# Moving the split activations of a float32r two-block network by 128 bytes in SBUF

## The chip, the cores and the metric

The kernel runs on one core of one Trainium2 chip. The metric is the device time of one execution in microseconds (us), lower is better. Everything is float32 in memory; the large products run on the matrix engine as float32r, in three passes.

## The reference: two transformer-like blocks

One sequence of 256 tokens of width 1024 goes through two blocks, with two layers each. The parts that matter here are all products of an activation with a weight:

```python
# first block, for each of 2 layers
h = h + 0.5 * (1 + mod2) * swiglu(u, ffn1_wg, ffn1_wu, ffn1_wd)     # 1024 -> 2816 -> 1024
proj = u @ w_in                      # retention, stick-breaking attention, mamba2
h = h + (1 + mod5) * (concat([y_ret, y_sb, y_ssm]) @ w_out)
h = h + 0.5 * (1 + mod8) * swiglu(u, ffn2_wg, ffn2_wu, ffn2_wd)
# second block, for each of 2 layers
proj = h @ w_in                      # neighbourhood, MLA and GQA attention, three gates
x = x + g_m * (merged @ w_out)
x = x + g_f * ((silu(gate) * up) @ ffn_w_down)
```

Each u is an RMS norm of the state, scaled and shifted by vectors that come from a conditioning vector times the matrices ada_w (the "ada" work).

## The kernel before

**Layout.** Activations stand transposed: 128 features on the partitions, the 256 tokens along the free dimension, one tile of 256 columns (1024 bytes) for each 128 features. A weight tile is 128 x 128 (512 bytes per partition) and is the stationary operand; the activation tile of 256 columns is the moving one. The exception is `tokens()`, for values that must stand untransposed: there a 128-column piece of the activation is stationary and the weights move.

**Three passes.** Each number is split into a high float32r part and a low one (the rest). `mm3` adds three matmuls into one PSUM tile: high weight by high activation, high by low, low by high. All of them are recorded at line L647 (`mm`). Each matmul has a weight load of its own.

**Weights.** 310 fills of up to 1 MB come through SP's queue into `ring`, a ring of 3 slots of 2048 floats per partition. A fill holds two "grains" of 1024 floats. For each grain ScalarE writes the high part into `high` (L1127) and VectorE the low part into `low` (L1561); both rings have 4 grains. TensorE works through the grains in order, 24 matmuls for a grain of eight 128 x 128 tiles. A fill is issued when the fill three before it has been split.

**Split activations.** The moving operands stand in five buffers, each the high parts followed by the low parts:

- `u_split`: the normed input of every projection, and of gate and up in the feed-forward stages
- `hid`: the hidden tiles of a feed-forward stage (22 high, 22 low)
- `xa` and `xr`: what goes into w_out of the first block (`into_acc`)
- `merged`: what goes into w_out of the second block (`into_acc`, the same function and the same weight tiles)

`u_split` ends at the byte `TOP`; `region`, a work area of `REGION` floats that the stages share, lies below it. `xa`, `xr`, `merged` and `hid` are views into `region` at fixed offsets:

```python
REGION = 16672
XA_AT, XR_AT, HID_AT = 12576, 6176, REGION - 2 * FT * T
TOP = 229312
...
self.u_split = self.sb("u_split", 2 * KT * T, F32R, TOP - 8 * KT * T)
base = TOP - 8 * KT * T - 4 * REGION
self.region = self.sb("region", REGION, F32, base)
self.xa = self.sb("xa", 16 * T, F32R, base + 4 * XA_AT)
```

**Stages.** In order: f1, m1, f2 for each layer of the first block, a final norm, then m2, f3 for each layer of the second, and an output norm. A feed-forward stage is 22 units of gate and up (48 matmuls each) and 528 matmuls of down. The mixers m1 and m2 put small float32 matmuls of attention and scan (the "side" pieces) between their projections. VectorE also does the ada products (L1543) at a fixed rate per grain.

The functions that the diff touches, with the profile's line numbers:

Of the kernel before, what the change touches and what calls it, by code (L numbers as in the profile page):

```python
# [24 lines left out]
T = 256  # L25
TT = T // P
LAYERS = 2
FF = 2816
FT = FF // P
CHUNK = 64  # L30
HD = 128
SSM_H, SSM_P, SSM_G, CONV = 8, 64, 2, 4
EPS = 1e-6
TRI = T + P
# [36 lines left out]

FIRST = 2 * KT
FIRST_AT = TT * D
REGION = 16672
XA_AT, XR_AT, HID_AT = 12576, 6176, REGION - 2 * FT * T


TOP = 229312

# [2 lines left out]
class Fill:  # L84


    def __init__(self, *parts):
        self.parts = parts
        _, _, _, self.rows, _, self.cols = parts[0]
        self.width = sum(rows * cols for _, _, _, rows, _, cols in parts)  # L90
        self.grains = []
# [334 lines left out]
class Memory:  # L426


    def __init__(self, nc, ctx):
        self.nc, self.at = nc, (nc.sbuf_base + 31) // 32 * 32  # L430
        names = ["pe", "act", "dve", "pool", "params", "ident", "const", "c", "cb", "x", "bias", "store", "const2"] \
            + [f"fill{i}" for i in range(SLOTS)] + [f"ada{i}" for i in range(ADA_SLOTS)] + [f"first{i}" for i in range(FIRST // 2 - 1)]
        self.sems = {n: ctx.enter_context(nc.semaphore(f"s_{n}")) for n in names}
        self.ring = self.sb("ring", SLOTS * SLOT)
        self.high = self.sb("high", GRAINS * GRAIN, F32R)
        self.low = self.sb("low", GRAINS * GRAIN, F32R)
        self.ada_ring = self.sb("ada_ring", ADA_SLOTS * D)
        self.cst = self.sb("cst", max(C1_W, C2_W))
        self.par = self.sb("par", BASE_C + PC_W)
        self.h = self.sb("h", KT * T)  # L440
        self.tmp = self.sb("tmp", 5 * 512)
        self.rope_t = self.sb("rope_t", 2 * 512)
        self.sil = self.sb("sil", 2 * T)
        self.rs = self.sb("rs", 2 * 512)
        self.ones = self.sb("ones", P)
        self.eps = self.sb("eps", 1)
        self.cond = self.sb("cond", 2 * D)
        self.sums = self.sb("sums", KT * len(JOBS))
        self.mods = self.sb("mods", KT * len(JOBS))
        self.gates = self.sb("gates", KT)  # L450
        self.gcol = self.sb("gcol", KT)
        self.dts = self.sb("dts", 8 * 16)
        self.keys = self.sb("keys", 4 * T)
        self.stat = self.sb("stat", 24)
        self.u_split = self.sb("u_split", 2 * KT * T, F32R, TOP - 8 * KT * T)
        base = TOP - 8 * KT * T - 4 * REGION
        assert self.at <= base, (self.at, base)
        self.region = self.sb("region", REGION, F32, base)
        self.xa = self.sb("xa", 16 * T, F32R, base + 4 * XA_AT)
        self.xr = self.sb("xr", 8 * T, F32R, base + 4 * XR_AT)  # L460
        self.merged = self.sb("merged", 16 * T, F32R, base)
        self.hid_split = self.sb("hid", 2 * FT * T, F32R, base + 4 * HID_AT)
        self.psum = ctx.enter_context(nc.psum_tensor("bank", [P, 8 * 512], F32))
        self.banks = [self.psum[:, i * 512:(i + 1) * 512] for i in range(8)]
        self.hv = tiles(self.h, KT)
        self.uh, self.ul = tiles(self.u_split, KT), tiles(self.u_split, KT, T, KT * T)
        self.squares, self.normed = tiles(self.tmp, 4), tiles(self.tmp, 4, T, 1024)
        self.hid = tiles(self.hid_split, FT), tiles(self.hid_split, FT, T, FT * T)
        self.x = self.reg(0, TT, D)


        self.xp = self.reg(0, 8, T + CONV - 1)
        self.rqk, self.sv, self.sg = self.reg(0, 4, 512), self.reg(2080, TT, 512), self.reg(3104, 4)
        self.sqk, self.sz, self.ry = self.reg(4128, 2, 512), self.reg(5152, 4), self.reg(5152, 2)
        self.xbc, self.xdt = self.reg(XR_AT, 8), self.reg(8224, TT, 512)
        self.cbm = [self.region[:, 9248 + g * TRI:9248 + (g + 1) * TRI] for g in range(SSM_G)]
        self.rr = [self.region[:, 10016 + i * TRI:10016 + (i + 1) * TRI] for i in range(2)]
        self.dec = [self.region[:, 10784 + i * TRI:10784 + (i + 1) * TRI] for i in range(2)]
        self.sy = self.reg(11552, 4)
        self.y_sb = tiles(self.xa, 8), tiles(self.xa, 8, T, 8 * T)  # L480
        self.y_ret = tiles(self.xr, 4), tiles(self.xr, 4, T, 4 * T)
        self.tb = [self.tmp[:, i * TRI:(i + 1) * TRI] for i in range(6)]
        self.dt8 = [self.dts[:, i * 16:(i + 1) * 16] for i in range(8)]


        self.qa, self.va = self.reg(0, 2), self.reg(1024, TT)

        self.ka, self.gkz = two(self.keys[:, :], 4), self.reg(512, 2)
        self.kr, self.cqn, self.ckvn = self.reg(2048, 1), self.reg(2560, 2), self.reg(3072, 1)
        self.qb, self.kb, self.vm = self.reg(3328, 4), self.reg(4352, 4), self.reg(5376, TT)  # L490
        self.gq, self.gk, self.gv = self.reg(5888, 4), self.reg(6912, 1), self.reg(7424, TT, P)

        self.gate2, self.o = self.reg(7680, 24), self.reg(13824, 8)
        self.total = self.reg(7680, 8)
        self.head_squares = [self.sil, self.rs[:, 512:1024]]
        self.inner = tiles(self.sil, 2)[:, 0, :], tiles(self.sil, 2)[:, 1, :]
        self.na_bias = self.region[:, 11776:13824]
        self.S = [self.tmp[:, i * 512:(i + 1) * 512] for i in range(3)]
        self.PT = [self.tmp[:, 1536:2048], self.tmp[:, 2048:2560], self.region[:, 15872:16384]]
        self.merged_hl = tiles(self.merged, 8), tiles(self.merged, 8, T, 8 * T)  # L500
# [62 lines left out]
def tiles(t, n, width=T, at=0):  # L563
    return t[:, at:at + n * width].rearrange("p (n w) -> p n w", n=n)


def two(ap, n=2):
    return ap.rearrange("p (n w) -> p n w", n=n)
# [1750 lines left out]
```

## Time and profile before

| what | value |
|---|---|
| time, median of 3 runs | 2097.65 us (2094.57 to 2100.68) |
| the profiled execution's own time | 2095.65 us |
| its span, first to last instruction | 2093.9 us |
| mean granted TensorE clock | 0.979 of full speed |
| TensorE matmul busy | 95% of the span, 15720 instructions |
| VectorE, ScalarE, GpSimd busy | 69%, 49%, 6% |
| DMA | 466.35 MB, mean 223 GB/s |

A matmul's duration in the trace (279 ns, say) is longer than the distance between two of them, since they are pipelined: what a stretch costs is read from the starts. A busy share near 100% therefore says that TensorE had no gap, not how fast it went.

### The profile page before, as it was taken

To read this page: it belongs to the slowest core of one execution; us is meant where nothing else is said; L and a number is where in the kernel's file an instruction comes from. 1 tells how busy PE (TensorE), PEld (TensorE's weight loads), DVE (VectorE), ACT (ScalarE), POOL (GpSimd) and SP (SyncE) were. 2 spreads that over 40 slices of the span, in tenths; PEclk is the share of its full clock that TensorE was granted. 3 is DMA by queue.
4 is the path that set the end of the run, shared out by engine and by line. 5 is a ranking of instruction groups with operands and counts; after the bars stand their busy time and mean duration, and the time that the engine had idled before them with its cause. 6 is when DMAs were issued, how large, how long until landed. Compare 5 with 4: busy or idle time off the path is not lost.

```text
span 2093.9 us, 37422 instructions
## 1 busy us (share of the span) xinstructions
PE 1988.4 (95%) x15720; PEld 1936.4 (92%) x15720; DVE 1437.9 (69%) x2203; ACT 1021.2 (49%) x1568; POOL 117.2 (6%) x113
## 2 busy tenths in 40 slices
PE   3999899989999999999999979998999899999999
PEld 3999899989999999999899979998999899989998
DVE  6767687877677676968776757665777776656554
ACT  3444556454545444664644455443545454525443
POOL 0000002200000000022000010000000100000000
PEclk8999999999999999999999989999999999999999
DMA  8777565567786775755577745455677664554552
GB/s 347 263 253 288 185 231 193 191 220 251 253 290 212 253 275 212 252 199 208 208 267 254 278 165 202 164 211 201 211 257 277 220 207 170 194 202 168 192 184 100
DMA packets 83848, 466.35 MB, mean 223 GB/s; under 512 B 9440, under 2 KB 9568, under 8 KB 44512
## 3 DMA queue, kind: packets, MB, share of 16 engines
q1 hardware_dynamic: 46496, 326.00, 43.5%
q10 hardware_dynamic: 37184, 137.97, 18.2%
q8 instruction: 123, 2.02, 0.4%
q14 instruction: 45, 0.37, 0.0%
HBM read 462.88 MB, written 1.05 MB: 222 GB/s over the span
## 4 chain that ended last, share of the span: by engine, by line
PE 85%; DVE 7%; ACT 4%; DMA 1%; issue 1%; POOL 1%; ACTq 0%; DVEq 0%
PE bank L647 84%; DVE low L1561 2%; DMA region<-ada 1%; DVE ada_ring L1543 1%; ACT high L1127 1%; DVE u_split L1604 1%; PE bank L916 1%; DVE tmp L1599 1%; ACT u_split L1165 0%; POOL region L2047 0%; DVE region L1975 0%; DVE region L1930 0%; ACT rs L1148 0%; PE bank L1055 0%; ACTq L1495 0%
## 5 line engine op out<-in xcount | busy, mean ns | idle before, releaser
L647 PE MATMUL bank<-u_split,high 128*128 128x256 f32 x6464 | 1171.2, 284 | 47.9 <-DVE u_split L1604 41.8
L647 PEld LDWEIGHTS bank<-u_split,high 128*128 128x128 f32 x6464 | 1000.2, 190 | 58.7 <-DVE u_split L1604 35.4
L1561 DVE TENSOR_TENSOR low<-ring,high 128x1024 fp32r<-128x1024 f32 (+1 forms) x600 | 732.6, 1229 | 393.4 <-issue 237.9
L647 PE MATMUL bank<-u_split,low 128*128 128x256 f32 x3232 | 909.6, 281 | 0.0
L1127 ACT ACTIVATE high<-ring 128x1024 fp32r<-128x1024 f32 (+1 forms) x600 | 602.5, 1045 | 108.3 <-PE bank L647 96.6
L647 PEld LDWEIGHTS bank<-u_split,low 128*128 128x128 f32 x3232 | 612.5, 190 | 0.4
L647 PE MATMUL bank<-hid,high 128*128 128x256 f32 x2112 | 373.4, 279 | 0.0
L647 PEld LDWEIGHTS bank<-hid,high 128*128 128x128 f32 x2112 | 322.4, 188 | 0.0
L1543 DVE SCALAR_TENSOR_TENSOR ada_ring<-ada_ring,cond 128x1024 f32<-128x1024 f32 x242 | 298.0, 1232 | 0.0
L647 PE MATMUL bank<-hid,low 128*128 128x256 f32 x1056 | 294.8, 279 | 0.0
L647 PEld LDWEIGHTS bank<-hid,low 128*128 128x128 f32 x1056 | 198.1, 188 | 0.0
L1193 ACT ACTIVATE sil<-bank 128x256 f32<-128x256 f32 x132 | 50.7, 384 | 276.2 <-PE bank L647 276.1
L1199 ACT ACTIVATE hid<-sil 128x256 fp32r<-128x256 f32 x132 | 55.4, 420 | 95.9 <-DVE sil L1651 95.9
L2017 POOL TENSOR_TENSOR tmp<-tmp 128x256 f32<-128x256 f32 x36 | 26.6, 740 | 1243.9 <-ACT tmp L1181 1243.9
L1181 ACT ACTIVATE tmp<-h 128x256 f32<-128x256 f32 x48 | 20.0, 418 | 136.4 <-DVE h L1639 136.4
L647 PE MATMUL bank<-region 128*128 128x256 f32 (+2 forms) x312 | 70.1, 351 | 4.6 <-DVE xa L1672 3.7
L647 PE MATMUL bank<-high,u_split 128*128 128x256 f32 (+1 forms) x384 | 68.1, 279 | 1.0 <-ACT region L1228 1.0
L647 PE MATMUL bank<-region,ring 128*128 128x256 f32 (+1 forms) x304 | 66.8, 380 | 0.0
L1599 DVE SCALAR_TENSOR_TENSOR tmp<-h,gcol,rs 128x256 f32<-128x256 f32 x88 | 40.8, 479 | 36.5 <-ACT rs L1151 36.5
L647 PEld LDWEIGHTS bank<-region 128*128 128x128 f32 (+1 forms) x312 | 53.6, 189 | 13.1 <-DVE xa L1672 4.3
L647 PEld LDWEIGHTS bank<-region,ring 128*128 128x128 f32 (+1 forms) x304 | 56.7, 187 | 9.1 <-ACT region L1473 0.5
L647 PEld LDWEIGHTS bank<-high,u_split 128*128 128x128 f32 x384 | 59.0, 189 | 1.3 <-ACT region L1335 1.2
(186 smaller groups left out, 1650.1 us busy)
## 6 DMA issues: line engine op xcount, KB each, us to landing
ring<-stream SPq DMA_DIRECT2D x302, 1024.0 KB, 5.5
ada_ring<-ada ACTq DMA_DIRECT2D x242, 512.0 KB, 4.3
region<-ada ACTq DMA_DIRECT2D x7, 1024.0 KB, 22.3
ring<-stream SPq DMA_DIRECT2D x4, 640.0 KB, 4.6
region<-na_bias ACTq DMA_DIRECT2D x2, 1024.0 KB, 5.5
ring<-stream SPq DMA_DIRECT2D x4, 512.0 KB, 4.2
cst<-const ACTq DMA_DIRECT2D x1, 1600.0 KB, 21.0
cond<-cond SPq DMA_DIRECT2D x2, 512.0 KB, 7.6
```

The costliest lines, as they stand in the source:

```text
L647: return pe.e.matmul(out, lhs, rhs, start=start, stop=stop, skip_group_check=True)
L916: t = pe.e.transpose(b[:, k * T + a * P:k * T + (a + 1) * P], m.S[p][:, a * T + k * P:a * T + (k + 1) * P], m.c2("ident"))
L1127: act.e.activation(hi, src, ACT.Copy).then_inc(*act.done(("high", n)))
L1181: act.e.activation(m.squares[:, square_slot(d), :], m.hv[:, d, :], ACT.Square) \
L1193: act.e.activation(g, m.banks[act.bank("hid", f, n)][:, 0:T], ACT.Silu).then_inc(*act.done(("silu", f, n)))
L1199: act.e.activation(m.hid[0][:, n, :], g, ACT.Copy).then_inc(*act.done(("hid_high", f, n)))
L1543: dve.e.scalar_tensor_tensor(out=w, in0=w, scalar=1.0, in1=m.cond[:, block * D:(block + 1) * D], op0=ALU.mult, op1=ALU.mult, accum_out=m.s ...
L1561: dve.e.tensor_tensor(lo, src, hi.bitcast(F32), ALU.subtract).then_inc(*dve.done(("low", n)))
L1599: dve.e.scalar_tensor_tensor(out=out, in0=m.hv[:, d, :], scalar=gain[:, d:d + 1], in1=m.rs[:, 0:T], op0=ALU.mult, op1=ALU.mult).then_inc(* ...
L1604: dve.e.scalar_tensor_tensor(out=m.ul[:, e, :], in0=m.normed[:, e % 4, :], scalar=m.mod(shift)[:, e:e + 1], in1=m.uh[:, e, :].bitcast(F32) ...
L2017: pool.e.tensor_tensor(total, total, m.squares[:, square_slot(d), :], ALU.add) \
```

## The change

It moves buffers and nothing else. Only addresses change; every engine's instructions, their order, their shapes and their waits are the same, line by line (one blank line less in the file puts each line number one lower).

```diff
-REGION = 16672
-XA_AT, XR_AT, HID_AT = 12576, 6176, REGION - 2 * FT * T
-
-
-TOP = 229312
+REGION = 16704
+XA_AT, XR_AT, HID_AT = 12608, 6208, REGION - 2 * FT * T
+
+TOP = 229184
...
-        self.xbc, self.xdt = self.reg(XR_AT, 8), self.reg(8224, TT, 512)
-        self.cbm = [self.region[:, 9248 + g * TRI:9248 + (g + 1) * TRI] for g in range(SSM_G)]
-        self.rr = [self.region[:, 10016 + i * TRI:10016 + (i + 1) * TRI] for i in range(2)]
-        self.dec = [self.region[:, 10784 + i * TRI:10784 + (i + 1) * TRI] for i in range(2)]
-        self.sy = self.reg(11552, 4)
+        self.xbc, self.xdt = self.reg(XR_AT, 8), self.reg(8256, TT, 512)
+        self.cbm = [self.region[:, 9280 + g * TRI:9280 + (g + 1) * TRI] for g in range(SSM_G)]
+        self.rr = [self.region[:, 10048 + i * TRI:10048 + (i + 1) * TRI] for i in range(2)]
+        self.dec = [self.region[:, 10816 + i * TRI:10816 + (i + 1) * TRI] for i in range(2)]
+        self.sy = self.reg(11584, 4)
```

The start of each buffer, in bytes from the start of a partition, and what is left of it after division by 256 and by 1024. Every tile of an activation lies a multiple of 1024 bytes behind its buffer's start, every 128-column weight tile a multiple of 512.

| buffer | before | mod 256 | mod 1024 | after | mod 256 | mod 1024 |
|---|---|---|---|---|---|---|
| high (weights) | 41088 | 128 | 128 | 41088 | 128 | 128 |
| low (weights) | 57472 | 128 | 128 | 57472 | 128 | 128 |
| u_split | 212928 | 192 | 960 | 212800 | 64 | 832 |
| hid | 167872 | 192 | 960 | 167744 | 64 | 832 |
| xa | 196544 | 192 | 960 | 196416 | 64 | 832 |
| xr | 170944 | 192 | 960 | 170816 | 64 | 832 |
| merged, region | 146240 | 64 | 832 | 145984 | 64 | 576 |

The distance of an activation from the weights, modulo 256, was 192 - 128 = 64 for all but `merged` and becomes 64 - 128 = -64, that is 192, for all. The parts of `region` at fixed offsets (`sv`, `sz`, `o`, `gate2` and others) move by 256 bytes; `xbc`, `xdt`, `cbm`, `rr`, `dec` and `sy` move by 128.

## Rows read from the trace of the kernel before

**Rows 1.** The page's first part: engine, busy us (share of span), instructions.

```profile
PE 1988.4 (95%) x15720; PEld 1936.4 (92%) x15720; DVE 1437.9 (69%) x2203; ACT 1021.2 (49%) x1568; POOL 117.2 (6%) x113
```

**Rows 2.** Longest pieces of the chain that ended last: start us, us, what.

```profile
41.28 188.34 PE bank L647 x1584
...
430.70 10.74 PE bank L647 x64
444.12 188.30 PE bank L647 x1584
643.90 181.19 PE bank L647 x1536
...
1018.57 9.36 PE bank L647 x64
1030.60 188.33 PE bank L647 x1584
...
1467.16 188.37 PE bank L647 x1584
...
1894.28 188.34 PE bank L647 x1584
```

**Rows 3.** Timeline of TensorE in m1's w_out: start us, us, what.

```profile
393.23 0.28 PE L647 MATMUL bank<-xa,low 128*128 128x256 f32 x1
393.35 0.40 PE L647 MATMUL bank<-xa,high 128*128 128x256 f32 x2
...
398.53 0.28 PE L647 MATMUL bank<-xa,low 128*128 128x256 f32 x1
```

**Rows 4.** The same in m2's w_out.

```profile
1447.82 0.28 PE L647 MATMUL bank<-merged,low 128*128 128x256 f32 x1
1447.93 0.39 PE L647 MATMUL bank<-merged,high 128*128 128x256 f32 x2
...
1460.74 0.28 PE L647 MATMUL bank<-merged,low 128*128 128x256 f32 x1
```

**Rows 5.** Matmuls by tile, whole span: duration ns min/median/max, first and last start.

```profile
L647 PE MATMUL bank<-hid,high x2112: 279/279/280, 167.3 to 2082.2; 128*128 128x256 f32 x192
L647 PE MATMUL bank<-xa,high x256: 278/279/681, 392.6 to 1009.9; 128*128 128x256 f32 x128
L647 PE MATMUL bank<-merged,high x256: 276/276/582, 1431.9 to 1887.7; 128*128 128x256 f32 x128
```

**Rows 6.** Tile u_split moving, windows 45:166, 885:902 and 337:342.5.

```profile
L647 PE MATMUL bank<-u_split,high x687: 279/279/280, 44.8 to 166.0; 128*128 128x256 f32 x172
...
L647 PE MATMUL bank<-u_split,high x93: 276/276/363, 885.5 to 901.9; 128*128 128x256 f32 x93
...
L647 PE MATMUL bank<-u_split,high x32: 276/276/363, 337.2 to 342.5; 128*128 128x256 f32 x32
```

**Rows 7.** Tile u_split stationary (tokens), windows 934:948, 873:882 and 1675:1684.

```profile
L647 PE MATMUL bank<-high,u_split x64: 276/276/369, 934.7 to 947.8; 128*128 128x256 f32 x64
...
L647 PE MATMUL bank<-high,u_split x53: 281/281/281, 872.8 to 882.0; 128*128 128x256 f32 x53
...
L647 PE MATMUL bank<-high,u_split x32: 279/281/281, 1677.1 to 1682.7; 128*128 128x256 f32 x32
```

**Rows 8.** Busy time by windows: window, us, engines, clock, DMA share, GB/s.

```profile
45.00:165.00 120.00, 120.00 (x1021) 120.00 (x1020) 83.38 (x120) 60.37 (x89) 0.00 (x0) 1.00 0.71 251
170.00:228.00 58.00, 58.00 (x495) 58.00 (x494) 41.98 (x53) 25.09 (x30) 4.45 (x6) 1.00 0.74 268
...
840.00:964.00 124.00, 119.37 (x966) 116.55 (x966) 100.18 (x166) 72.75 (x102) 15.68 (x15) 1.00 0.62 226
```

**Rows 9.** Waits of SP's own queue in 60:160: us in total, times, longest.

```profile
SPq L350 <- DVE low L1561: 92.7, 35, 3.8
```

**Rows 10.** The chain by line, in 237:375, 375:431, 964:1018 and 1225:1427.

```profile
by line: PE bank L647 78.4%; DVE low L1561 3.8%; ACT L1228 1.9%; DVE ada_ring L1543 1.7%; ACT high L1127 1.5%; issue 1.4%; ACT L1231 0.9%; ACT L1238 0.9%; ACT region L1228 0.9%; ACT region L1323 0.9%; DVE region L1753 0.8%; DVE region L1747
...
by line: DVE low L1561 25.2%; DVE ada_ring L1543 16.8%; issue 9.5%; ACT high L1127 7.1%; POOL region L2047 5.3%; DVE rope_t L1786 3.3%; ACT xa L1259 3.1%; DVE region L1801 2.9%; DVE region L1759 2.9%; DVE region L1794 2.8%; ACT xr L1300 2.6
...
by line: DVE low L1561 29.1%; DVE ada_ring L1543 12.7%; issue 10.5%; ACT high L1127 7.3%; POOL region L2047 5.5%; DVE rope_t L1786 3.4%; ACT xa L1259 3.2%; DVE xa L1672 3.1%; DVE region L1801 3.0%; DVE region L1759 3.0%; DVE region L1794 2.
...
by line: PE bank L647 89.4%; PE bank L916 3.5%; DVE u_split L1604 1.5%; DVE tmp L1599 1.4%; ACT L1139 0.6%; DVE low L1561 0.6%; ACT u_split L1165 0.5%; issue 0.4%; DVE region L1975 0.3%; DVE region L1930 0.3%; ACT region L1440 0.3%; ACT h L
```

## The prediction

> **What bounds the kernel now.** I read the page first. TensorE is busy for 95% of the span, VectorE for 69%, ScalarE for 49% [rows 1]. The longest pieces of the chain that ended last are six feed-forward stages, in each of which nothing but matmuls stands on the path: five of 1584 matmuls in 188.3 us and one, cut a little shorter, of 1536 in 181.19 [rows 2]. The last is 118.0 ns a matmul; the others come to 118.9 with their start. A busy engine without gaps can still be slow, so the question is what one matmul costs, and whether it costs the same from every buffer. For that I read the timeline at the two places where the same function (`into_acc`) works with the same weight tiles on different activations.
>
> - From `xa`, a triple of matmuls (one low row each) comes 15 times between 393.23 and 398.53 [rows 3]: 5.30 / 45 = 117.8 ns a matmul.
> - From `merged`, it comes 38 times between 1447.82 and 1460.74 [rows 4]: 12.92 / 114 = 113.3 ns.
>
> The difference is 4.4 ns, or 3.8%, with the engine full in both. The duration of one matmul is a marker for the two paces: 276 ns in `merged`, 279 and more in `xa`, and in all 2112 of `hid` [rows 5], whose minimum is 279. So every down product runs at the slow pace. Gate and up do too: 687 matmuls from 45 to 166 with a minimum of 279 [rows 6].
>
> **The rule I take from it.** `xa`, `xr`, `hid` and `u_split` stand 64 bytes above the weights modulo 256; `merged` alone stands 64 below. The change gives the four the place of `merged`, modulo 1024 too (832), so each new pairing of a moving tile and a stationary one has a precedent in this trace. It is not a pure function of the address: `u_split` at its old place also ran at 276 ns in some stretches, as 93 matmuls at 885 and 32 at 337 [rows 6]. A timeline of the whole span gives about 420 such matmuls among 3360 of the mixers' projections, and none in the feed-forward stages. So there are two paces, a stretch falls into one of them when it starts, and the address sets the odds: at the old place some 70 stretches between two breaks, of which about one in seven ran fast, in whole or in part; at the place of `merged`, four stretches, all fast within two triples of their start, two of them after a start at the low clock. For `tokens()` the roles are swapped (weights move at 128, `u_split` is stationary at 192, so the moving operand is 64 below as in `merged`): 276 ns at 934, but 281 at 873 and at 1677 [rows 7]. Counted out, some 410 of 560 were fast. This is what keeps me from certainty.
>
> What a page says goes against the change. The Trainium skill's "SBUF — State Buffer" (Who interferes with whom) gives TensorE two independent read ports, one for the moving operand and one for weight loads, and says that it never waits on anyone; its "TensorE: Matmul & The Clock Gate" (Back-to-back issue gap) makes a warm gap of N/2.4 + 2.5 ns, an estimate of 109.2 for 256 columns, without a word on addresses. By them the change would be worth nothing. This trace shows neither that gap nor one gap for all buffers, and the measurement decides; what is left of the rule is a rival below.
>
> **The sum, by part.** Price per matmul that goes from slow to fast: 4.4 ns. Its bounds: 0 if the pace doesn't depend on the place; no more than 4.4 from any row of a 128 x 128 by 256 matmul, since 113.3 is the fastest pace a long stretch shows; and on the other side a small loss, since 281 ns [rows 7] against 279 [rows 5] is the slowest marker that any full stretch shows. I take 4.4, as `merged` is the nearest row: same function, same weights, same residue.
>
> - Feed-forward, six stages: 6 x 1584 = 9504 matmuls x 4.4 = 41.8 us, all on the path [rows 2]. The cover: VectorE is busy 83.4 of 120 us in gate and up and 42.0 of 58 in down [rows 8]; with 4% less time that is 72% and 75%. DMA share is 0.71 to 0.74 at 251 to 268 GB/s, which would be some 260 to 279. SP's queue spends 92.7 of 100 us waiting for a slot to be split, no wait over 3.8 [rows 9]: weights are there before they are needed. If that cover were gone, all 41.8 would be.
> - Projections of the mixers: 3360 matmuls with `u_split` moving, less 144 narrow ones, less 420 already fast, less 192 in the windows 375:431 and 964:1018, leaves 2600. In those two windows the chain is VectorE's (low 25 and 29%, ada 17 and 13%, L647 not among the leading lines) [rows 10], so a faster TensorE there only waits longer. Elsewhere L647 is 78 to 89% of the chain [rows 10], so I count 9 in 10: 2600 x 0.9 x 4.4 = 10.3 us. In the densest one, VectorE is at 100.2 of 124 us [rows 8], 81%, and would be at 83%.
> - `xa` and `xr`: 576 matmuls. They lie in the VectorE-bound windows but for the last 64 of each layer, which are on the path [rows 2]: 128 x 4.4 = 0.6 us.
> - `tokens()`: the swapped roles now have the moving weights 64 above `u_split`. At worst all 410 fast ones turn slow, 410 x 4.4 = -1.8 us; at best they keep their pace. I take -1.0.
> - `merged`: its residue modulo 256 stays, modulo 1024 it moves to 576, for which there is no precedent. At worst 384 x 4.4 = -1.7 us. I take 0.
> - `xdt`, `rr`, `dec`, `cbm`, `xbc` and `sy` move by 128 bytes against the constants. Their float32 matmuls are some hundred on the path; even at 4.4 ns each that is 0.5 us either way, counted at 0. The writes of VectorE and ScalarE into the moved buffers keep their 64-byte alignment: 0. No DMA's destination changes modulo 256: 0.
>
> Sum: 41.8 + 10.3 + 0.6 - 1.0 = 51.7. The profiled execution took 2095.65 us, 2.0 below the median, so its twin would take 2043.9 and the median 2046.0: **2046 us**, 2.5% less.
>
> **Rivals.** About 0.3% (6.3 us) is what a measurement of this kernel can tell from no change.
>
> 1. *Only part of it goes fast.* A stretch picks its pace at its start, and a feed-forward stage is one long stretch: each stage that stays slow costs 7.0 us. For it: `tokens()` at the same distance stayed slow over whole stretches. Against it: `merged` was fast four times in four, twice after a start like that of a feed-forward stage. With three of six stages slow, and half of the mixers' part: 2046 + 21 + 5 = 2072. Chance 0.17.
> 2. *Nothing changes.* Two independent read ports (the rule above), and `merged` fast for another reason than its place, as what the other engines do just then, or what ran before it. For it: `u_split` fast at the old place at 885 and 337. Against: the same buffer at the same distance is slow for all of 9504 feed-forward matmuls. Time: 2091 to 2104. Chance 0.13.
> 3. *Slower.* A third pace. The projections and `hid` read tiles further from the weights than `merged` does; if there the two reads met more often than now, by one more step of 4.4 ns, 13,000 matmuls would give +57 us, 2155. It decides from 0.5 ns a matmul on (6.3 us over 13,000). The trace shows no full stretch slower than 281 ns. The losses that it does show possible (`tokens`, `merged`, and the 420 lucky ones of `u_split`) add up to 5.3 us and stay under the bound. Chance 0.05.
> 4. *More than that,* a pace under 113.3, or feed-forward stages whose ends profit too: under 2038. Chance 0.02.
>
> **How the numbers follow.** The forecast has 0.63. Its own range runs from 2038 (every split matmul of the mixers on the path, 57 us) to 2056 (a fifth of the sum lost to waits of VectorE). The range for 8 in 10 takes in the first rival: 2038 to 2092. Faster: 0.63 + 0.17 + 0.02 = 0.82; the same 0.13; slower 0.05.
>
> **What the profile after would show.** `hid,high` with a median of 276 ns instead of 279, and `u_split` too; the five chain pieces of 1584 at about 181.3 us instead of 188.3, the piece from 643.90 at about 174; `xa` and `xr` at 276 with no gain in their windows; `tokens()` mixed or at 279 to 281; VectorE's busy time unchanged at 1438 us, its share 70 to 71%. The prediction is wrong if `hid` stays at 279 (rival 2), if stages differ among each other (rival 1), if `hid` shows 282 or more (rival 3), or if it shows 276 while waits of L647 for `low` or for `ring` grow by as much as the pace gives.

## The result, and the profile after

The changed kernel takes 2066.23 us (median of 4, 2059.43 to 2082.15) against 2096.66; the ratio is 0.9872, with a 95% interval of 0.9844 to 0.9899. That is 1.3% faster where 2.5% was forecast, inside the range of 2038 to 2092, and nearest to the first rival (only part of the stretches goes fast, 2072). The profiled execution took 2068.39 us, its span 2066.6. Three executions of later kernels took 2229, 3632 and 6857 us and are left out of the ratios below.

The page's first part, as in [rows 1]:

```profile
PE 1958.1 (95%) x15720; PEld 1905.4 (92%) x15720; DVE 1438.2 (70%) x2203; ACT 1020.5 (49%) x1568; POOL 116.3 (6%) x113
```

TensorE's busy time fell by 30.3 us; the other engines' hardly moved. VectorE's is what it was, 1438, and its share rose by the shorter span. The six long pieces of the chain that ended last answer to [rows 2]:

```profile
41.22 181.51 PE bank L646 x1584
...
436.89 188.34 PE bank L646 x1584
629.63 189.25 PE bank L646 x1584
...
1023.79 183.62 PE bank L646 x1584
...
1458.52 174.38 PE bank L646 x1536
...
1878.85 176.52 PE bank L646 x1536
```

Six stages that were alike are now of three kinds. The first is fast throughout (181.5 us for 1584, 7 less than before) and so is the fifth (174.4 for 1536, where 181.2 had been the price). The second and third are as slow as ever. The fourth and sixth gained about two thirds of what the first did. The matmuls' durations tell where, by tile in the windows of the third, fourth and fifth stage (ns min/median/max, first and last start; two windows for the fourth):

```profile
L646 PE MATMUL bank<-u_split,high x704: 280/281/552, 629.6 to 756.3; 128*128 128x256 f32 x176
L646 PE MATMUL bank<-hid,high x352: 280/281/282, 756.5 to 818.5; 128*128 128x256 f32 x176
...
L646 PE MATMUL bank<-u_split,high x704: 275/276/416, 1023.8 to 1145.0; 128*128 128x256 f32 x176
...
L646 PE MATMUL bank<-hid,high x262: 281/281/282, 1160.9 to 1207.0; 128*128 128x256 f32 x131
...
L646 PE MATMUL bank<-hid,high x160: 276/276/277, 1572.9 to 1599.9; 128*128 128x256 f32 x160
```

276 ns is the fast pace of 113.3 ns a matmul, as it was for `merged` in [rows 5]. At the new place the slow pace of 117.8 ns shows as 281, not 279. The third stage was slow from its start. The fourth was fast in gate and up and slow in down. Here is the place where it changed, TensorE's timeline:

```profile
1150.35 0.39 PE L646 MATMUL bank<-hid,high 128*128 128x256 f32 x2
1150.58 0.28 PE L646 MATMUL bank<-hid,low 128*128 128x256 f32 x1
1150.69 0.41 PE L646 MATMUL bank<-hid,high 128*128 128x256 f32 x2
1150.93 0.28 PE L646 MATMUL bank<-hid,low 128*128 128x256 f32 x1
1151.05 0.40 PE L646 MATMUL bank<-hid,high 128*128 128x256 f32 x2
1151.29 0.28 PE L646 MATMUL bank<-hid,low 128*128 128x256 f32 x1
```

A row of two high matmuls takes 0.39 before 1150.69, 0.41 there, and 0.40 from then on; the triples come every 0.34 us before and every 0.35 after. The starts of the two matmuls at 1150.69 lie 124 ns apart instead of 113. It is the 49th matmul of the down product, the first of its third weight grain. VectorE's timeline at that moment:

```profile
1149.31 2.36 DVE L1560 TENSOR_TENSOR low<-ring,high 128x1024 fp32r<-128x1024 f32 x2 [2.03 <-ACT high L1126]
```

The low part of that grain ended half way through these 2.36 us, at 1150.54, 0.15 us before the 49th matmul started. One hiccup of 11 ns, and the next 479 matmuls ran 4.4 ns slower each: 2.1 us. The sixth stage shows the same 124 ns at the same matmul; the first stage shows 125 there, a second of 122 three matmuls later, and stayed fast.

The traces of the experiments below bear this out. In all traces at distances 64 and 192, this one included, 24 down products came fast to their third grain with its low part ended only 143 to 157 ns before the 49th matmul; in every one a distance of 121 to 133 ns follows, and behind it 12 were fast and 12 slow. In seven others, each the fifth stage of its trace, the low part had ended 256 to 265 ns before; no such distance appears, and all seven stayed fast.

Where the 27.3 us of the span came from: counted from the first to the last matmul of each stage, the feed-forward stages gave 6.8 + 0 - 1.0 + 4.7 + 6.9 + 4.7 = 22.1. The third lost 1.0 us by its start, and not by its pace: its first matmuls fell into a stretch of half clock, which the same stage of the kernel before had not met. The granted clock is the third figure from the end in these rows of the windows view, 0.70 after (first row) and 1.00 before:

```profile
629.00:639.00 10.00, 9.37 (x59) 9.40 (x60) 9.23 (x18) 7.60 (x12) 0.00 (x0) 0.70 0.18 59
...
636.00:646.00 10.00, 8.44 (x65) 8.16 (x66) 9.11 (x18) 8.02 (x13) 0.00 (x0) 1.00 0.15 52
```

What lies between the stages, mixers above all, gave 0.3, 0.6, 4.2 and -0.1 us, 5.0 in all. By count, outside the two windows bound by VectorE, 1712 matmuls with `u_split` moving were fast after 416 before, which would be 5.7 us; `tokens()` lost 128 fast ones (0.6 us) and `merged` 196 (0.9).

### The profile page after: what moved, and what is told of

It reads as the page before. It is cut to its first block, busy times and chain, and to the rows that moved or that the text cites. A ratio compares the mean times of both kernels' runs of the same rounds, so it can differ in the third digit from the quotient of the medians.

```text
span 2066.6 us, 37422 instructions
## 1 busy us (share of the span) xinstructions
PE 1958.1 (95%) x15720; PEld 1905.4 (92%) x15720; DVE 1438.2 (70%) x2203; ACT 1020.5 (49%) x1568; POOL 116.3 (6%) x113
## 4 chain that ended last, share of the span: by engine, by line
PE 84%; DVE 8%; ACT 4%; DMA 2%; issue 1%; POOL 1%; ACTq 0%; DVEq 0%; SPq 0%
PE bank L646 83%; DVE low L1560 3%; DVE ada_ring L1542 1%; DMA region<-ada 1%; ACT high L1126 1%; DVE u_split L1603 1%; PE bank L915 1%; DVE tmp L1598 1%; DMA ring<-stream 0%; ACT u_split L1164 0%; POOL region L2046 0%; DVE region L1974 0%; DVE region L1929 0%; ACT rs L1147 0%; DVE region L1690 0%
## 5 line engine op out<-in xcount | busy, mean ns | idle before, releaser
L646 PE MATMUL bank<-u_split,high 128*128 128x256 f32 x6464 | 1147.9, 283 | 50.2 <-DVE u_split L1603 43.7
L646 PE MATMUL bank<-hid,high 128*128 128x256 f32 x2112 | 368.3, 279 | 0.0
```

Of the source, the lines that this page charges most:

```text
L646: return pe.e.matmul(out, lhs, rhs, start=start, stop=stop, skip_group_check=True)
```

## The experiments

Twelve experiments ran in three sets, one of them the changed kernel again; each time is set against the kernel before on the same chip. A *stretch* is a row of matmuls without a break between them; it has *settled* when its distances stay at one level. Where exactly a break is drawn moves the counts of stretches by a few.

**Theory A**: TensorE's pace depends on the distance, modulo 256, between the moving operand and the stationary one; it sets the odds with which a stretch settles at 113.3 or at 117.8 ns. **Theory B**: the mix of stages is a lottery, or comes from something else, and the distance doesn't touch it.

**First set: the distance.** From the changed kernel, one line each:

```diff
-TOP = 229184
+TOP = 229248        # distance 0
+TOP = 229312        # distance 64, merged too
+TOP = 229120        # distance 128
```

> All split activations, merged too, stand at 128 modulo 256, exactly where the weights' parts stand (distance 0). Theory A (the distance modulo 256 sets the odds with which a stretch of matmuls settles at 113.3 or at 117.8 ns; 64 is poor, 192 better): the pace differs from both kernels; if equal residues are the worst case, no stretch at 276 ns and some 2098 to 2101 us (before had 320 fast matmuls of merged and about 410 of tokens: losing them costs up to 3 us). Theory B (a lottery that the addresses don't touch, in which after drew well): 2060 to 2100 us, any mix of stages.

> The distance of before (64) for all, merged included. Theory A: the feed-forward stages stay at 279 to 280 ns, merged goes from 276 to 279, the time is that of before plus 0 to 2 us (2097 to 2100). Theory B: some feed-forward stages at 276 ns and a time as of after, 2060 to 2085.

> All split activations at 0 modulo 256, 128 away from the weights' parts. Theory A gives no number for this distance: between the two kernels, 2060 to 2097, if the odds change evenly with the distance, and possibly all fast (2046) if 128 is the farthest point of a circle of 256. Theory B: as after.

> The changed kernel once more, unchanged. Theory A and B both: 2059 to 2082 us, as its four executions; the question is which feed-forward stages are fast. Under a lottery at each start the stages at 276 ns are others than in the first trace (there the first and fifth whole, the fourth and sixth for gate and up, the second and third not); if the same ones are fast again, what runs before a stage decides and not chance.

| distance | ratio to before | 95% interval | mean pace, ns | stretches of u_split that settled fast |
|---|---|---|---|---|
| 0 | 1.0165 | 1.015 to 1.018 | 119.9 | 0 of 68 |
| 64, all | 1.0015 | 0.9993 to 1.0037 | 117.4 | 12 of 68 |
| 128 | 1.0094 | 1.0068 to 1.0119 | 118.7 | 0 of 69 |
| 192, again | 0.9834 | 0.9814 to 0.9853 | 114.6 | 52 of 71 |

The pace is the mean of all distances between two neighbouring three-pass matmuls, breaks left out; in the kernel before it was 117.5 with 5 of 68, in the first trace of the changed kernel 115.3 with 44 of 71. Theory B is dead: 2128 to 2132 us at distance 0, 2110 to 2120 at 128 and 2060 to 2062 at 192 don't overlap, and neither 0 nor 128 has a single fast stretch. Distance 0 is slower than anything in the trace of before, 2130.5 us, and the long pieces of its chain say so:

```profile
41.21 192.22 PE bank L646 x1584
...
451.18 191.81 PE bank L646 x1584
647.39 192.84 PE bank L646 x1584
...
1049.72 193.03 PE bank L646 x1584
```

My guess for it, 2098 to 2101, had only taken the fast stretches away and was off by 30 us: there are more paces than two. Distance 128 missed as well: I had expected it between the two kernels or faster, and it is slower than both. At distance 64 `merged` lost what had led me to the forecast. By tile:

```profile
L646 PE MATMUL bank<-merged,high x256: 276/279/582, 1431.8 to 1886.1; 128*128 128x256 f32 x128
```

The median went from 276 in [rows 5] to 279. The repeat of the changed kernel (2059.8 and 2061.9 us) drew otherwise: the second, third and fourth stage were fast in gate and up and the sixth was slow, where in the first trace the sixth had been fast and the second and third slow. So which stage is fast is not fixed by the program alone. It isn't an even lottery either: the first and the fifth stage were fast in gate and up in all seven traces at distance 192, those of the next two sets included.

**Second set: whose place counts, and how locally.** The weights moved instead of the activations, in the kernel before; `hid` alone left at the old distance, in the changed kernel; and the two distances between:

```diff
         self.ring = self.sb("ring", SLOTS * SLOT)
+        self.at += 128
```

```diff
-XA_AT, XR_AT, HID_AT = 12608, 6208, REGION - 2 * FT * T
+XA_AT, XR_AT, HID_AT = 12608, 6208, REGION - 2 * FT * T - 32
```

```diff
-TOP = 229184
+TOP = 229152        # distance 160
+TOP = 229216        # distance 224
```

> The kernel before, its activations where they were, but the weights' parts (and all buffers behind them) 128 bytes higher, at 0 modulo 256: the distance of u_split, hid, xa and xr becomes 192, that of merged 64. Theory A (only the distance counts): feed-forward stages at 276 ns in some or most, merged at 279 and more, 2058 to 2082 us. Theory B (the activations' own place counts, 64 good and 192 bad): all as before, hid at 279, merged at 276, 2094 to 2100 us.

> The changed kernel with hid alone left at its old distance of 64. Theory A: gate and up settle fast in some stages, as in the changed kernel, but nearly all down products run at 117.8 ns, since a stretch that comes fast from u_split meets the old distance: the changed kernel's two traces had 1.9 and 3.6 stages' worth of fast down products of six, 528 x 4.4 = 2.3 us each, so about 6 us over the changed kernel, 2065 to 2085. Rival C (a stretch keeps the pace that it settled at, whatever comes): hid stays fast wherever u_split is, and the time is that of the changed kernel, 2058 to 2082.

> All split activations at distance 160. Found so far: 119.9 ns at 0, 117.8 (7 to 9% fast) at 64, 118.7 at 128, and 113.3 with 117.8 mixed at 192. If the pace follows the distance smoothly, 160 lies between 128 and 192: some 115 to 117 ns, 2070 to 2105 us. If what counts is a whole step of 64 bytes, 160 acts like 128 (2110 to 2120) or like 192 (2058 to 2082).

> All split activations at distance 224, between 192 and 256, which is 0. Smooth: some 115 to 118 ns, 2070 to 2110 us. By steps of 64: like 192 (2058 to 2082) or like 0 (2128 to 2132). If the reads of weight and activation must not meet within a window, 192 may be its edge, and 224 all fast at 113.3: about 2040 to 2046.

*Weights moved*: 2069.03 us, ratio 0.988 (0.9849 to 0.9911), although every activation stands where it stood before. The chain of that kernel:

```profile
41.21 183.79 PE bank L648 x1584
...
440.26 181.50 PE bank L648 x1584
626.16 184.77 PE bank L648 x1584
...
1017.96 181.53 PE bank L648 x1584
...
1444.39 181.48 PE bank L648 x1584
...
1863.99 188.34 PE bank L648 x1584
```

Five of six stages are fast, in whole or through gate and up. It is the distance that counts, not the place of the activations; nor is it the weights' place, since the first set left that alone.

*`hid` left*: 2078.48 us, ratio 0.9924 (0.9898 to 0.995). By tile, in gate and up of the third stage and in its down part:

```profile
L646 PE MATMUL bank<-u_split,high x674: 276/276/384, 639.8 to 754.4; 128*128 128x256 f32 x169
...
L646 PE MATMUL bank<-hid,high x322: 279/280/280, 759.9 to 816.6; 128*128 128x256 f32 x161
```

Five stages were fast in gate and up, and all 3168 matmuls of `hid` were slow. The crossing in the third stage, TensorE's timeline:

```profile
754.27 0.39 PE L646 MATMUL bank<-u_split,high 128*128 128x256 f32 x2
754.50 0.28 PE L646 MATMUL bank<-u_split,low 128*128 128x256 f32 x1
754.61 0.40 PE L646 MATMUL bank<-hid,high 128*128 128x256 f32 x2
754.85 0.28 PE L646 MATMUL bank<-hid,low 128*128 128x256 f32 x1
```

Rival C, a pace that a stretch keeps whatever comes, is out. There is no gap at the crossing: the distance to the first matmul of `hid` is 113 ns and the next one 118 or 119, in all five cases. So the distance acts at once. What a crossing the other way does, from 64 to 192 without a gap, no run shows.

*160 and 224*: 2109.84 us (1.0064, 1.0041 to 1.0087) and 2107.63 (1.0064, 1.004 to 1.0088). Their mean pace is 118.3 for each, outside both of the ranges that I had called smooth (the time of 224 lies inside its range, that of 160 does not), and no stretch of `u_split` settled fast (0 of 69, 0 of 68). At 160 a stage still draws its pace: the mean of a stage's settled part was 118.7 in the first two, 120.0 in the third and 117.3 in the last three. 192 is a narrow spot: 32 bytes to either side it is gone. Two limits of this scan: 160 and 224 are also the only places off the 64-byte grid, which no run separates from their distance, and 32 and 96 weren't run. And that 256 bytes is the period, not 512, rests on `merged` alone: after the change it is 448 from the weights modulo 512, where the others are 192, and 8 of its 12 stretches were fast in the three traces with it there (the changed kernel twice, `hid` left).

**Third set: what throws a stretch into the fast pace.** In the four traces at distance 192, a stretch that came slow to narrow weight loads (96 or 8 columns, as in the projections `kr` and `dt`) was fast behind them, 5 times of 5. So six extra matmuls, whose result is overwritten, go in at two places of each feed-forward stage:

```diff
                 r, g = grain(what, f, n)
+                if n == 1 and i == 0:
+                    for _ in range(2):
+                        mm3(b[0:96, 0:T], [x[:, 0, 0:96] for x in g], (m.uh[:, 0, :], m.ul[:, 0, :]), True, False)
                 for k in range(KT):
...
             pe.wait_ge(("hid_low", f, k))
+            if d == 1 and k == 0:
+                for _ in range(2):
+                    mm3(b[0:96, 0:T], [x[:, at % TILES, 0:96] for x in g], [x[:, 0, :] for x in m.hid], True, False)
             t = mm3(...)
```

The control has 128 for 96, the last kernel `range(1)`. The third has the first of the two insertions in the kernel before, with 8 columns and `range(6)`.

> The changed kernel plus six matmuls with a weight load of 96 columns, whose result is overwritten, at two places of each feed-forward stage (start of the second unit, start of the second down tile): 72 matmuls, 8.1 us if each costs 113 ns. Seen so far: at distance 192 every stretch that met a 96- or 8-column weight load at the slow pace was fast within 5 matmuls (5 of 5), and stayed so. Theory N (a shorter weight load lets the slow pace go over into the fast one): all six stages at 276 ns behind each place, in the profile and in every timed run, time 2066 - 24 + 8 + 5 (mixers as before) = 2050 to 2058, with less spread than the changed kernel's 23 us. Rival L (each start or disturbance deals anew): stages mixed as before, time that of the changed kernel plus 8, 2067 to 2090.

> The control: the same 72 extra matmuls at the same places with full 128-column weight loads. Both theories: the stages keep the mix of the changed kernel, 2067 to 2090 us; if it is as fast as the 96-column form, it is not the shorter weight load that tips.

> The kernel before, at the old distance of 64, plus 18 matmuls with an 8-column weight load at the start of the second unit of each of the six feed-forward stages (108 matmuls, some 12.5 us). At the old place, too, stretches became fast behind 8-column loads (4 of 4 within 17 matmuls) and no fast stretch fell back. Theory A2 (the address sets only how a stretch gets into the fast pace; once in, it stays at either place): gate and up and down at 276 ns in all six stages, 2097 - 40 + 12 = 2069 us. Rival A3 (at the old distance the fast pace holds only for short stretches and is lost in a long one): hid at 279 in most stages, 2095 to 2110.

> As the first, with three extra matmuls per place instead of six (36, 4.1 us). Theory N: if three narrow weight loads are enough to tip, 2046 to 2054 us and all stages fast; if it takes the four or five seen in the traces, some stages stay slow and the time is 2055 to 2075.

| kernel | us | ratio | 95% interval |
|---|---|---|---|
| six of 96 columns, twice a stage | 2060.11 | 0.9829 | 0.981 to 0.9849 |
| six of 128 columns (control) | 2071.23 | 0.9894 | 0.9856 to 0.9932 |
| 18 of 8 columns, old place | 2092.08 | 0.9973 | 0.9954 to 0.9991 |
| three of 96 columns | 2060.91 | 0.9834 | 0.9804 to 0.9865 |

The second insertion of the second stage in the first kernel, TensorE's timeline:

```profile
568.46 0.28 PE L646 MATMUL bank<-hid,low 128*128 128x256 f32 x1
568.58 0.40 PE L646 MATMUL bank<-hid,high 128*128 128x256 f32 x2
568.82 0.28 PE L646 MATMUL bank<-hid,low 128*128 128x256 f32 x1
568.93 0.39 PE L646 MATMUL bank<-hid,high 128*96 128x256 f32 x2
...
569.99 0.39 PE L646 MATMUL bank<-hid,high 128*128 128x256 f32 x2
570.22 0.28 PE L646 MATMUL bank<-hid,low 128*128 128x256 f32 x1
570.33 0.39 PE L646 MATMUL bank<-hid,high 128*128 128x256 f32 x2
570.56 0.28 PE L646 MATMUL bank<-hid,low 128*128 128x256 f32 x1
```

It comes in slow (0.36 us from 568.46 to 568.82) and leaves fast (0.34 from 570.22 to 570.56). In the down parts this happened in 4 of 4 stages that came slow with six narrow matmuls and in 2 of 2 with three. With full-width loads it happened in 0 of 2, and six down products of the other kernels at this distance that turned slow at the 49th matmul stayed slow to their end. So the narrow load does it, not the extra matmul: theory N holds there. The six narrow matmuls have a distance of 124 ns just behind them in the four slow cases; the three have none above 120, so no gap is needed. The time says the same: the six narrow and the six full-width matmuls, on one chip, gave 2058 to 2066 and 2067 to 2084 us, with intervals that don't overlap. At the start of the second unit it did worse, and the reason is the second finding. The control's third stage, TensorE's timeline:

```profile
630.98 0.39 PE L646 MATMUL bank<-u_split,high 128*128 128x256 f32 x2
631.21 0.28 PE L646 MATMUL bank<-u_split,low 128*128 128x256 f32 x1
631.32 0.44 PE L646 MATMUL bank<-u_split,high 128*128 128x256 f32 x2
631.60 0.28 PE L646 MATMUL bank<-u_split,low 128*128 128x256 f32 x1
631.72 0.40 PE L646 MATMUL bank<-u_split,high 128*128 128x256 f32 x2
631.95 0.28 PE L646 MATMUL bank<-u_split,low 128*128 128x256 f32 x1
```

The stage had already been fast (0.39 for a pair). At 631.32 there is a gap of 162 ns where the second unit begins, and behind it the stretch is slow (0.40), for the rest of the stage. In the 96-column kernels such a gap (121 to 153 ns) fell into the extra matmuls in nine of the twelve stages; seven of these went on fast and two slow. My insertion stood at the place that deals anew, not behind it. So rival L is half right: a gap deals anew, and a narrow load without a gap tips the slow pace into the fast one. The median, 2060.1, stayed above my 2050 to 2058. In the profiled execution one stage ran slow through gate and up, but that was the slowest of the four (2066.35); what kept the others above isn't known. Three narrow matmuls were enough to tip, and yet 2060.9 missed the 2046 to 2054 that I had put on that, for the same reason: one stage fell slow at the second unit.

At the old place only 2 of 5 stages that came slow went fast behind 18 narrow matmuls, where I had counted on all; one more arrived fast. All three then held it for 1000 matmuls. Two lost it at the 49th of the down product, with a gap of 129 and 131 ns, and stayed slow to the end of the stage; the third met no gap and kept it. So A2 is right that the fast pace is stable at distance 64, and wrong in what it leaves out: after a gap only about one stretch in eight settles fast there. The time, 2092.1, lies between A2's 2069 and A3's 2095 to 2110. Nor is a narrow load a sure way at this distance: of the four slow stretches that met 96-column loads in the mixers (the kernel before and the one with all at 64), one went fast.

The two kernels with narrow loads are 1.7% faster than before, the changed kernel 1.3% and, in its repeat, 1.7%. The intervals overlap, so it isn't shown that they beat it.

## Why the prediction was half right

**What bounds it and the price: right.** TensorE without gaps was the bound, and the price of 4.4 ns a matmul between the two paces was exact: 117.8 and 113.3 are the two levels of the changed kernel too. The marker of 276 ns worked. No cover broke: VectorE's share went to 70%, as forecast, and TensorE's waits for `u_split` and `low` grew from 60.9 to 63.6 us only.

**The step that failed** is the odds: "at the place of `merged`, four stretches, all fast within two triples of their start". From four out of four the prediction gave 0.63 to nearly every stretch being fast. In four traces at distance 192 (the changed kernel twice, weights moved, `hid` left), 196 of 285 stretches of `u_split` settled fast, 69%; at distance 64 it was 17 of 136, 12%. With 69% a stretch, the forecast's feed-forward term of 41.8 us should be some 29, and it measured 22.1, of which 1.0 was lost to the clock. The rows that spoke for this were on record: `tokens()`, at the same distance with the roles swapped, slow in two whole stretches [rows 7]. The first rival got 0.17 where the evidence, 4 of 4 beside about 410 of 560, called for at least as much as the forecast had. That a stage is one draw, or two, makes the time spread: 2059 to 2082 in the first four executions of the changed kernel. The kernel before, which also has a few fast stretches, took 2089 to 2101 in 37 of 39 executions on record and 2082.6 and 2087.3 in two. That the result came out near the first rival's 2072 is in part this lottery: another four executions could have a median some us away (the repeat took 2060 and 2062).

**What the prediction didn't see** is that the fast pace can be lost inside a stage. It treated a stage as decided at its start. A faster TensorE comes to the third grain of the down product just as VectorE finishes it, and 11 ns of waiting deal anew: twice in the first trace that cost 2.1 us. That the late grain causes the hiccup is read from the order of events, in 24 stages that have both and 7 that have neither; no run took that wait away.

**Terms.** Mixers with all their parts: forecast 10.3 + 0.6 - 1.0 = 9.9, measured 5.0, for the same reason. By count, the projections gave 5.7 of their 10.3. `tokens()`: forecast -1.0, counted -0.6; of its 480 matmuls of 256 columns, 321 to 460 were fast in the three traces with its old distance (the kernel before, all at 64, 18 narrow) and 47 to 284 in the seven with its new one, so distance matters with the roles swapped too, but with other odds. `merged`: counted 0 in the forecast, and it lost 0.9, as three of its four stretches were slow. Two other traces with `merged` at exactly this place (the repeat, and `hid` left) have 3 of 4 and 4 of 4 fast, so its new place modulo 1024 isn't needed to explain it. `xa` and `xr` turned fast in 10 of 12 stretches and gave little, as said, since VectorE bounds their windows. One slip in the working: 2038 as the lower end of the forecast takes the 57 us off the profiled execution; off the median they give 2041.

**The rival of no change**, drawn from the rule that TensorE's two read ports don't disturb each other (the Trainium skill, "SBUF — State Buffer", Who interferes with whom), is refuted by nine kernels that differ in addresses alone and whose medians lie between 2066 and 2131 us. The 109.2 ns beside it is a formula that its page (the Trainium skill, "TensorE: Matmul & The Clock Gate", Back-to-back issue gap) gives for an isolated matmul and not for a stream with a weight load for each, so 113.3 and 117.8 ns don't contradict it.

What stays open: the mechanism behind the paces. The runs show that the distance between the two operands matters and that a shorter weight load helps, which fits two reads that meet or miss each other; nothing here shows the memory itself.

## What to carry to other kernels

- Where TensorE is full, divide the time of a long gapless stretch by its matmuls, for each buffer, and compare. A difference of 4% between buffers with the same shapes was worth 1.3 to 1.7% of this kernel, and moving a buffer by 128 bytes added no instruction. Scan all distances from the weights; neighbours of a good one can be bad.
- Count draws, not matmuls. A long stretch that holds its pace is one observation, and four such are too few to call something certain.
- Behind a gap a stretch may settle at another pace, so a wait of 11 ns can cost 2 us. Look at the places where a faster TensorE will arrive first: here a low part that was ready 0.26 us ahead was early enough, and one ready 0.15 us ahead was not. That widening the margin pays is an expectation; no run did it.

## What the runs showed of the hardware that I had not expected

- With 128 x 128 weights and 256 moving columns, both float32r, the mean distance between matmuls was 119.9 ns at an address distance of 0 modulo 256, 117.4 to 117.5 at 64, 118.7 at 128, 118.3 at 160, 114.6 to 115.3 at 192 and 118.3 at 224, breaks and half-clock stretches left out. For the whole kernel that is 1.0165 of the time before at 0 against 0.9834 and 0.9872 at 192.
- At distances 64 and 192 the pace has two stable levels, 113.3 and 117.8 ns, each held for over 1500 matmuls; which one is settled within some six matmuls after a gap. Where the distance went from 192 to 64 without a gap, the pace went from 113 to 118 ns at the first matmul, 5 times of 5.
- A gap as short as 11 ns was followed by a change from the fast level to the slow one. Three or six matmuls with 96-column weight loads were followed by the change back in 6 of 6 cases in the down product at distance 192; six with full-width loads in 0 of 2.
